# A denoising step on one core: in the early phase each unit's main products are put ahead of the next eighth's pair of chunks on TensorE

## The reference, cut to what matters

```
shift, scale, gate = split(silu(cond) @ w_ada + b_ada, 3)     # w_ada: 2048 x 6144
h = rmsnorm(x, g) * (1 + scale) + shift
q, k, v, z = split(h @ w_in, 4)                               # layer 0, w_in: 2048 x 8192
```

## Time and profile before

| | us |
|---|---|
| median of 3 runs | 1109.95 |
| lowest, highest | 1106.69, 1114.34 |
| the profiled execution, its own time | 1111.23 |
| its span, first to last instruction | 1109.4 |
| TensorE busy, of the span | 1057.1 (95%) |
| VectorE busy | 766.9 (69%) |
| ScalarE busy | 542.2 (49%) |
| early phase, first product of unit 0 to first product of unit 24 | 31.1 to 143.0 |

### The profile page before, as it was taken

The page is one execution under the profiler, slowest core; times in us unless marked ns, Lnnn a source line. Parts: engine busy times, 40 slices in busy tenths (PEclk is TensorE's granted clock), DMA queues, the critical chain, the costliest instruction groups (busy, mean ns, idle before and its releaser), DMA issues.

```text
span 1109.4 us, 18584 instructions
## 1 busy us (share of the span) xinstructions
PE 1057.1 (95%) x7426; PEld 825.4 (74%) x7426; DVE 766.9 (69%) x1206; ACT 542.2 (49%) x762; POOL 226.7 (20%) x382
## 2 busy tenths in 40 slices
PE   2999899999999999999999989999999989999996
PEld 2777677777777777777777768888787877878885
DVE  2665585766576667766788866369997997476664
ACT  5343545444433344445444465566758376454442
POOL 1010330432043403320233240200221322100000
PEclk9999999999999999999999989999998999999999
DMA  9999968999799979995799986977583958764552
GB/s 378 419 419 420 372 262 318 354 352 344 282 342 403 363 278 346 333 369 183 285 370 352 340 323 235 283 220 250 194 266 105 305 195 298 287 249 163 189 197 95
DMA packets 62406, 325.61 MB, mean 293 GB/s; under 512 B 8208, under 2 KB 14992, under 8 KB 30192
## 3 DMA queue, kind: packets, MB, share of 16 engines
q1 hardware_dynamic: 42944, 267.93, 64.4%
q0 software_dynamic: 12176, 45.33, 11.9%
q10 hardware_dynamic: 7200, 11.16, 2.8%
HBM read 296.04 MB, written 28.34 MB: 292 GB/s over the span
## 4 chain that ended last, share of the span: by engine, by line
PE 75%; DVE 12%; DMA 6%; ACT 3%; issue 2%; POOL 1%; SPq 0%; DVEq 0%; ACTq 0%; POOLq 0%
PE ps L852 20%; PE ps L854 19%; PE ps L853 19%; PE ps L717 5%; DMA early<-in_wada 4%; DVE wlo L1535 4%; PE ps L975 2%; DVE sb L1651 2%; PE ps L736 2%; DVE sb L1663 2%; DMA araw<-in_wadag 1%; DVE t L1648 1%; PE ps L791 1%; PE ps L774 1%; ACT whi L1136 1%
## 5 line engine op out<-in xcount | busy, mean ns | idle before, releaser
L1535 DVE TENSOR_TENSOR wlo<-raw,whi 128x1024 fp32r<-128x1024 f32 x284 | 347.0, 1225 | 235.0 <-ACT whi L1136 230.4
L1136 ACT ACTIVATE whi<-raw 128x1024 fp32r<-128x1024 f32 x284 | 299.3, 1058 | 399.4 <-PE ps L854 368.4
L852 PE MATMUL ps<-whi,xhi 128*128 128x512 f32 x1136 | 461.8, 407 | 13.8 <-DVE wlo L1535 11.8
L853 PE MATMUL ps<-wlo,xhi 128*128 128x512 f32 x1152 | 451.8, 392 | 0.0
L854 PE MATMUL ps<-whi,xlo 128*128 128x512 f32 x1136 | 445.7, 392 | 0.0
L852 PEld LDWEIGHTS ps<-whi,xhi 128*128 128x128 f32 x1136 | 214.7, 189 | 90.8 <-issue 21.2
L854 PEld LDWEIGHTS ps<-whi,xlo 128*128 128x128 f32 x1136 | 214.4, 189 | 47.4
L853 PEld LDWEIGHTS ps<-wlo,xhi 128*128 128x128 f32 x1152 | 218.0, 189 | 40.9
L717 PE MATMUL ps<-araw,cT 128*32 128x512 f32 x512 | 61.5, 597 | 0.8 <-DMA araw<-in_wadag 0.8
L1663 DVE TENSOR_TENSOR sb<-sb,t 128x128 f32<-128x128 f32 x140 | 49.4, 357 | 4.6
L1553 DVE TENSOR_TENSOR xlo<-ps,xhi 128x512 fp32r<-128x512 f32 x40 | 27.4, 688 | 15.0 <-ACT xhi L1157 14.7
(11 more groups left out here) (233 smaller groups left out, 1077.1 us busy)
## 6 DMA issues: line engine op xcount, KB each, us to landing
raw<-in_w SPq DMA_DIRECT2D x144, 1024.0 KB, 6.8
araw<-in_wadag SPq DMA_DIRECT2D x64, 1024.0 KB, 9.1
early<-in_wada SPq DMA_DIRECT2D x20, 1024.0 KB, 19.0
araw<-in_wada SPq DMA_DIRECT2D x12, 1024.0 KB, 16.8
btab_scratch<-bs ACTq DMA_DIRECT2D x32, 256.0 KB, 6.5
ctab_scratch<-ce POOLq DMA_DIRECT2D x16, 512.0 KB, 8.4
btab<-btab_scratch SPq DMA_DIRECT2D x16, 512.0 KB, 4.3
ctab<-ctab_scratch POOLq DMA_DIRECT2D x16, 512.0 KB, 4.7
```

The costliest lines, as they stand in the source:

```text
L852: mm(acc, xhi[:, kt, st], hi[:, k], start=kt == 0, stop=False)
L853: mm(acc, xhi[:, kt, st], wlo[:, slot, k0 % 2, k], start=False, stop=False)
L1136: af(whi_at(k).rearrange("p k c -> p (k c)"), src, ACT.Copy).then_inc(s_hi, 1)
L1535: tt(wlo[:, slot, k % 2].rearrange("p k c -> p (k c)"), src, whi_at(k).rearrange("p k c -> p (k c)").bitcast(F32), ALU.subtract).then_inc( ...
```

## The change

In TensorE's loop the call of `unit` moves up, ahead of the pair and of the finishing of the next eighth. No instruction is added or removed, and no other engine's program changes.

```diff
@@ -1028,13 +1028,13 @@
                     pe.wait_ge(s_bs, 2 * NQ)
                 for i, g in ahead(k):
                     transposed(i, g)
+                unit(k, b, u)
                 for p in range(2, N_EARLY // 2):
                     if k == pair_unit(p):
                         ada_early(p)
                 if eighth_at(k):
                     transposed(0, eighth_at(k))
                     early_columns(eighth_at(k))
-                unit(k, b, u)
                 attention(k, b)
                 tables(k)
                 modulation(b, u)
```

## The result

The changed kernel takes 1137.19 us (median of 4 runs, 1134.55 to 1140.66) against 1109.32 us before: ratio 1.0237, 95% interval 1.0207 to 1.0266, slower by 28 us. The profiled execution took 1136.35 us with a span of 1134.5, 25.1 us more than before.

The account below looks back on a forecast made before the run. The prediction held TensorE to bound the early phase, level with or a little behind full transfers. 15 us of added idle plus 6 us of half rate on 1109.95 us made 1131 us, range 1119 to 1141.

Parts of the forecast that it names:

- the forecast's own band of 1128 to 1134: Whole kernel: the span of times around the forecast of 1131 us, given a chance of 0.40.
- rival C: Early phase: the clock falls at every long gap and one or two short ones, 15 + 15, about 1140 us; chance 0.17.
- The bound: Early phase: TensorE and transfers both full, TensorE level with the transfers or a little behind, so new gaps lose time.
- rival A: Early phase: the transfers set the pace, so the kernel is not slower, 2.75 us gained, 1107 us; chance 0.08.
- The uncovered chains: Units 1, 4, ..., 19: waits from pair to next split lose their cover, adding 9.9 us at even eighths, 8.2 at odd.
- Unit 4: Ahead of unit 4: its split stands behind VectorE's 25 pole and factor operations, leaving TensorE idle for 3.75 us.
- The 0.4 us ahead of unit 10: Ahead of unit 10: its split stands behind VectorE's `c_table`, adding 0.4 us of idle time.
- The start: Kernel start: unit 0 runs early at half rate; pair 3 ends 2.6 us later, one more unit done, net about nothing.
- The idle part in sum: Early phase: all added idle time less waits removed, 15.8 or 13.9 us by two counts, taken as 15.
- The clock on top: Behind the early phase's long gaps: TensorE falls to half rate twice at 3.1 us each, 6.2 us in all.
- B, stalls alone: Early phase: only the idle time costs, with no fall of the clock, 15 us, 1125 us; chance 0.23.
- D, chains partly hidden: Unit 4's idle and half of that at even eighths vanish; 6 us and one fall, about 1118 us; chance 0.12.

Follow-up runs that it names:

- pairs only: Kernel before with only the swap at units 0, 3, ..., 18, each unit ahead of the first pair: 1110.03 us, ratio 0.9993.
- start busy: Kernel before plus 16 zero-weight dummy matmuls in the 4.4 us wait for chunk 4 at the start: 1112.38 us, ratio 1.0024.
- filled: Changed kernel plus 12 or 7 zero-weight dummy matmuls in the gaps at even or odd eighths, none ahead of unit 4: 1126.07 us, ratio 1.0140.
- the last of the three attempts: Kernel before with the swap at units 0, 3, ..., 18 only, two splits ahead and the pole operations moved to unit 3: 1114.91 us, ratio 1.0051.
- eighths only: Kernel before with only the swap at units 1, 4, ..., 19, ahead of pair, transposes and early_columns: 1132.40 us, ratio 1.0202.
- all-filled kernel: Changed kernel with 12 or 7 dummy matmuls in the gaps at even or odd eighths and 14 more ahead of unit 4: 1125.14 us, ratio 1.0130.
- half-filled kernel: Changed kernel with 6 or 3 dummy matmuls in the gaps at even or odd eighths, none ahead of unit 4: 1131.95 us, ratio 1.0191.

## Why the prediction was right, and where it was off

The median of 1137.19 lies inside the range, but above the forecast's own band of 1128 to 1134 and nearer to rival C's 1140.

**The bound: right.** TensorE and the transfers were both full, TensorE a little behind. The runs with an earlier start (pairs only, start busy) show it from the other side: TensorE's gains came back as waits for chunks. The rule by which the most used resource decides (rival A) failed, because the chain made the turn longer than the 13.7 us that the transfers need; they fell to a share of 0.43 between 136 and 152 us.

**The uncovered chains: right.** Computed from the two turns of the earlier trace rows, 3.3 and 2.05 us to add at even and odd eighths; measured gaps of 3.05 to 3.12 and 1.88 to 1.95 us, with the 0.2 us of modelled tail that I had allowed for. The wait of about 0.85 us ahead of unit 22 stayed (0.86), the one ahead of unit 23 and those for chunks went.

**Unit 4: the mechanism right, the size off.** 3.75 us computed, 2.37 measured, since TensorE itself came later, having run unit 2 partly at half rate. With the rate whole until then it was 3.54 us (filled). The 0.4 us ahead of unit 10 did not come.

**The start: right in sum.** Pair 3 ended at 38.8 instead of 39.4; unit 0 ran there at half rate.

**The idle part in sum: 15 us predicted, 14.0 measured** with every gap filled. Unit 24 was to start at about 158 with no fall; it started at 157.06.

**The clock on top: this is the step that failed.** The prediction has it as "Two falls: 6.2 us". There were seven falls, and they cost 11.1 us (25.1 less 14.0). Both factors were off: the number too low, the price of 3.1 us for each too high, since five of the seven lasted 3.4 us and not the 6.8 us of the earlier trace rows, and one of these was hidden by the wait ahead of unit 4. That they offset each other in part is luck. I had taken the gaps of 2.25 and 2.05 us that passed without a fall as a bound for the shorter ones, but those at the eighths fell at 1.88 us too. A pair and transposes stood ahead of these gaps and dense units ahead of 139.08, but no run shows this to be the reason. Against it speak a gap of 2.62 us behind a pair and transposes that passed without a fall (97.12 in the last of the three attempts), and one of 2.68 us between dense units that did not (start busy). The one row of my own that spoke of this, the fall at 844.18 after 1.84 us between sparse products, I had set aside. The same 2.37 us ahead of unit 4, without transposes, cost no fall.

The Trainium skill (TensorE: Matmul & The Clock Gate, "HAM oscillation — how this bites in real kernels") has a loop with a wait in every turn come back at half rate every time, with waits of some 3 to 5 us. The trace agrees, seven turns of seven, and after shorter waits, 1.9 to 3.1 us; eighths only had six of seven. I should have given this more than a rival's 0.17. Rival C had about the right number of falls, five or six, at the long price for each, and came to 1140; at the 1.6 us that the seven cost on average, they would have made 8 to 10 us on top of 15, an estimate close to the measured 25.1. The median lies 2.8 us further from before than the profiled execution does, whose 1136.35 is among the lower of its four runs.

**Rivals.** A, transfers set the pace: no. B, stalls alone: no; the all-filled kernel shows what they would have cost, 14 us. D, chains partly hidden: no, each gap had its full length.

## What to carry to other kernels

Before moving work ahead of the step that releases other engines, time the chain from that step to the next instruction that needs it and ask what fills it: work that looks merely "in front" may be the cover. Each engine's order is a part of it; the same order on TensorE cost 28 us with the splits behind the release and 5 with them ahead. Count a repeated gap twice, as idle time and as half rate behind it. The length of one gap does not tell whether the clock will fall, and repeated executions differ; so fill the gaps with dummy work once, to measure the two parts apart.

## What the runs showed of the hardware that I had not expected

- Half rate came at gaps of only 1.9 us behind a pair of 128-column products and transposes (seven of seven turns, and six of seven in eighths only, whose last 1.88 us passed), and not at 2.25 us between dense units at 139 us of the kernel before. Neither holds throughout: see the gaps of 2.62 and 2.68 us above. The stretches at half rate in the phase lasted 3.4 us or 6.8 us.
- A fall costs nothing where TensorE then waits for another engine: the one at 41.3 us was hidden in the wait ahead of unit 4.
- Matmuls with zero weights kept the clock at 1.00 as the real ones do.
- Repeated executions of the half-filled kernel spread over 11 us, and of start busy over 10, where pairs only stayed within 3.5; in the first two the mean clock was highest in the fastest execution (0.993 and 0.994) and lower in the slow ones (0.982 to 0.986, and 0.986).
